# Moving twelve of sixteen modulation weight blocks into the first projections of a GLA and forgetting-attention step

## The reference

```python
def ada_params(c, w, b, n):
    mod = jax.nn.silu(c) @ w + b
    return jnp.split(mod[:, None, :], n, axis=-1)
...
shift, scale, gate = ada_params(c, ada_w[layer], ada_b[layer], 3)
h = rms_norm(x) * (1 + scale) + shift
```

## Time and profile before

| | us |
|---|---|
| median of 3 runs | 3111.63 (3107.04 to 3114.2) |
| the profiled execution | 3111.56 |
| its span, first to last instruction | 3110.0 |
| TensorE busy | 2840.9 (91%) |
| DVE, ACT, POOL busy | 1485.1, 965.3, 790.9 |
| mean granted TensorE clock | 0.95 of full |

### The profile page before, as it was taken

The page is one execution under the profiler, slowest core; times in us unless marked ns, Lnnn a source line. Parts: engine busy times, 40 slices in busy tenths (PEclk is TensorE's granted clock), DMA queues, the critical chain, the costliest instruction groups (busy, mean ns, idle before and its releaser), DMA issues. The chain is left out here.

```text
span 3110.0 us, 41239 instructions
## 1 busy us (share of the span) xinstructions
PE 2840.9 (91%) x15730; PEld 2026.1 (65%) x15730; DVE 1485.1 (48%) x3498; ACT 965.3 (31%) x1579; POOL 790.9 (25%) x460
## 2 busy tenths in 40 slices
PE   4699999997999986999969999699999999994998
PEld 2377777775777865778857877455555555552667
DVE  2462332112877637541166105566666666653343
ACT  2321332211655544210043112134444434442000
POOL 1020000000000003000020000278887888785000
PEclk8799999998999998999989999699999999996999
DMA  8712222113566524221142231334314332314764
GB/s 302 272 68 72 81 65 85 72 45 130 171 218 196 163 93 182 82 75 49 48 174 82 49 72 52 94 110 117 92 37 110 113 96 59 91 32 158 223 214 125
DMA packets 281928, 355.22 MB, mean 114 GB/s; under 512 B 40044, under 2 KB 172460, under 8 KB 281681
## 3 DMA queue, kind: packets, MB, share of 16 engines
q1 hardware_dynamic: 279436, 344.30, 35.2%
q0 software_dynamic: 2304, 8.39, 0.8%
HBM read 250.28 MB, written 102.10 MB: 113 GB/s over the span
## 5 line engine op out<-in xcount | busy, mean ns | idle before, releaser
L2339 POOL TENSOR_TENSOR at_p_sum<-at_p_sum,at_p 128x1024 f32<-128x1024 f32 (+3 forms) x264 | 522.2, 1978 | 84.4 <-ACT at_p L2185 61.4
L2185 ACT ACTIVATE at_p<-psum 128x1024 f32<-128x1024 f32 (+1 forms) x320 | 270.2, 895 | 384.0 <-PE psum L2012 380.0
L2236 DVE CUSTOM_DVE_ANT_0 psum<-psum,at_f_wide 128x512 f32<-128x512 f32 (+3 forms) x640 | 376.9, 631 | 0.0
L717 POOL TENSOR_TENSOR kv_h_lo<-kv_aux,kv_h_hi 128x512 fp32r<-128x512 f32 x16 | 24.1, 1508 | 1015.6 <-ACT kv_h_hi L693 984.7
L2092 PE MATMUL psum<-at_p,at_v 128*64 128x512 f32 (+3 forms) x1280 | 270.5, 544 | 0.7 <-ACT at_p L2185 0.7
L806 PE MATMUL psum<-kv_w_hi,kv_h_hi 128*128 128x512 f32 x512 | 201.2, 393 | 13.1 <-DVE kv_w_lo L961 13.1
L806 PE MATMUL psum<-gla_w_hi,gla_h_hi 128*128 128x512 f32 x512 | 201.3, 393 | 10.7 <-DVE gla_w_lo L961 10.7
L808 PE MATMUL psum<-gla_w_hi,gla_h_lo 128*128 128x512 f32 x512 | 203.0, 397 | 0.0
L807 PE MATMUL psum<-gla_w_lo,gla_h_hi 128*128 128x512 f32 x512 | 202.2, 395 | 0.0
L807 PE MATMUL psum<-kv_w_lo,kv_h_hi 128*128 128x512 f32 x512 | 200.3, 391 | 0.0
L808 PE MATMUL psum<-kv_w_hi,kv_h_lo 128*128 128x512 f32 x512 | 200.0, 391 | 0.0
(11 more groups left out here) (431 smaller groups left out, 6111.1 us busy)
## 6 DMA issues: line engine op xcount, KB each, us to landing
mod_w<-in_ada_w SPq DMA_DIRECT2D x12, 2048.0 KB, 15.5
at_f_wide<-F SPq DMA_DIRECT2D x32, 512.0 KB, 5.4
at_page<-in_cache_k SPq DMA_DIRECT2D x32, 512.0 KB, 3.6
gla_w_raw<-in_gla_w_in SPq DMA_DIRECT2D x6, 2048.0 KB, 7.7
mod_x<-in_x_prompt SPq DMA_DIRECT2D x16, 512.0 KB, 15.9
mod_w<-in_kv_ada_w SPq DMA_DIRECT2D x4, 2048.0 KB, 12.3
v_gla<-gla_stage SPq DMA_DIRECT2D x32, 256.0 KB, 2.0
sg_gla<-gla_stage SPq DMA_DIRECT2D x32, 256.0 KB, 2.0
```

Source lines behind the costliest of these rows:

```text
L717: pool.tensor_tensor(part(h_lo, k, G), h_tmp[0], part(h_hi, k, G).bitcast(F32), ALU.subtract)\
L2185: act.activation(p_tile[e % PT][:, :, skip:NB], pair_of(bank_st[e % 2])[:, :, skip:NB], ACT.Exp)\
L2236: op = dve.tensor_tensor_reduce(pair_of(at(n))[:, a, 0:w], pair_of(at(n))[:, a, 0:w], f_wide[:, a, c * NB:c * NB + w], 1.0, -3.0e38, ALU.s ...
L2339: pool.tensor_tensor(p_sum[s][:, :, skip:NB], p_sum[s][:, :, skip:NB], p_tile[e % PT][:, :, skip:NB], ALU.add).then_inc(p_added, 1)
```

## The change

The modulation phase keeps blocks 0 to 3, the GLA layer's shift and scale. The other twelve are loaded and projected within blocks 1 to 4 of the GLA projections, three in each, through `w_raw`, with TensorE products after units 2, 6 and 10 and folds after units 3, 7 and 11, in PSUM bank 7. ACT copies the strips over part of `w_raw`; DVE adds the bias and writes `modT` or gate rows. The biases of the eight turned blocks come by eight loads into a tile `biasT`; gate biases come by a load each. The next projection's weights are loaded after unit 11 of a block rather than after unit 0 (for blocks 2 to 5). In the modulation phase the order of x changes: four tiles, then the next projection and the fold, with no look-ahead from one group of four to the next.

```diff
@@ modulation_phase
+    blocks = g.mod_blocks[0:g.MOD_FIRST]
@@ SP
-                for n in range(DEEP):
-                    load(n)
+                load(0)
+                sp.wait_ge(cleared, 1)
+                sp.dma_start(bias[0:NC, :], g.i.ada_b[0:1, 0:N * NB].broadcast_to([NC, N * NB])).then_inc(bias_loaded, 16)
+                for n in range(N):
                     load_x(n)
...
+                    if n + 1 < N:
+                        load(n + 1)
@@ PE
                 for n in range(N):
+                    for t in range(PER * n, PER * n + PER):
+                        turn_x(t)
                     if n + 1 < N:
                         project(n + 1)
-                    for t in range(PER * n, PER * n + PER):
-                        turn_x(t)
                     turn(n)
@@ DVE
                 for n in range(N):
-                    if n + 1 < N:
-                        gather(n + 1)
                     for t in range(PER * n, PER * n + PER):
-                        if t + 1 < g.NT:
+                        if (t + 1) % PER:
                             scale_x(t + 1)
                         dve.wait_ge(x_turned, 2 * t + 2)
                         dve.tensor_copy(g.xT[:, 4:8, t * P:(t + 1) * P], ps_x[1]).then_inc(x_kept[1], 1)
+                    if n + 1 < N:
+                        gather(n + 1)
                     keep(n)
+                    if n + 1 < N:
+                        scale_x(PER * n + PER)
...
+PROJECT_AT, FOLD_AT = (2, 6, 10), (3, 7, 11)
@@ projection_phase
+            mod_parts, gate_rows, gate_bias = w_raw[:, 0, :], w_raw[0:NC, 1, :], w_raw[0:NC, 2, :]
...
+        def mod_at(n, t, times):
+
+            return 3 * (n - 1) + times.index(t) if gate and 1 <= n <= 4 and t in times else None
+
+        def mod_load(sp, n, m):
+
+            if m % 3 == 0:
+                sp.wait_ge(w_ready, K * (n + 1) + K)
+                sp.wait_ge(s_made, n + 1)
+            w, j = g.mod_blocks[later[m]]
+            sp.dma_start(w_raw[:, :, :], col_blocks(w, j)).then_inc(mod_loaded, 16)
+
+        def mod_rest(sp, m):
+
+            b = later[m]
+            if b in g.mod_gates:
+                sp.wait_ge(mod_projected, m + 1)
+                sp.dma_start(gate_bias, g.mod_bias[b].broadcast_to([NC, NB])).then_inc(gate_bias_loaded, 16)
+            sp.wait_ge(mod_kept, m + 1)
+            if b in g.mod_gates:
+                sp.dma_start(g.mods[:, b * NB:(b + 1) * NB], gate_rows).then_inc(gate_rows_stored, 16)
+                sp.wait_ge(gate_rows_stored, 16 * gates_to(m))
+
+        def mod_project(pe, m):
+
+            pe.wait_ge(mod_loaded, 16 * m + 16)
+            if m:
+                pe.wait_ge(mod_kept, m)
+            in_strips(pe, g.bank[7], lambda k: g.cT[:, k, :], lambda k: w_raw[:, k, :]).then_inc(mod_projected, 1)
+
+        def mod_part(act, m):
+
+            act.wait_ge(mod_projected, m + 1)
+            act.activation(mod_parts, g.bank[7][:, :], ACT.Copy).then_inc(mod_parted, 1)
+
+        def mod_fold(pe, m):
+
+            pe.wait_ge(mod_parted, m + 1)
+            if later[m] in g.mod_gates:
+                mm = pe.matmul(g.bank[7][0:STRIP, :], g.fold[:, :], mod_parts, start=True, stop=True)
+            else:
+                for q in range(R):
+                    mm = pe.matmul(g.bank[7][:, q * NC:(q + 1) * NC], mod_parts[:, q * P:(q + 1) * P], g.fold[:, 0:NC],
+                                   start=True, stop=True)
+            mm.then_inc(mod_folded, 1)
+
+        def mod_keep(dve, m):
+
+            b = later[m]
+            dve.wait_ge(mod_folded, m + 1)
+            if b in g.mod_gates:
+                dve.wait_ge(gate_bias_loaded, 16 * gates_to(m))
+                dve.tensor_tensor(gate_rows, g.bank[7][0:NC, :], gate_bias, ALU.add).then_inc(mod_kept, 1)
+            else:
+                at = turned_blocks.index(b) * R
+                dve.wait_ge(mod_bias_fixed, 2)
+                dve.tensor_tensor(modT[:, b * R:(b + 1) * R, :], g.bank[7][:, 0:R * NC].rearrange("p (q c) -> p q c", c=NC),
+                                  biasT[:, at:at + R].unsqueeze(2).broadcast_to([P, R, NC]), ALU.add).then_inc(mod_kept, 1)
@@ SP, store_units
+                        if mod_at(p.base + j, t, FOLD_AT) is not None:
+                            m = mod_at(p.base + j, t, FOLD_AT)
+                            mod_rest(sp, m)
+                            if m % 3 < 2:
+                                mod_load(sp, p.base + j, m + 1)
+                            elif p.base + j + 1 < n_blocks:
+                                load_w(*all_blocks[p.base + j + 1])
@@ SP, prologue
                 if gate:
                     z_load(sp)
+                    for n, b in enumerate(turned_blocks):
+                        sp.dma_start(biasT[:, n * R:(n + 1) * R].rearrange("p (o q) -> p o q", o=1),
+                                     g.mod_bias[b].rearrange("a (q p) -> p a q", p=P),
+                                     allow_slow_non_contiguous=True).then_inc(mod_bias_loaded, 16)
                 sp.dma_start(x_in[0][0:NS, :], x_sample).then_inc(x_loaded[0], 16)
@@ PE, block_units
+                        if mod_at(n, t, FOLD_AT) is not None:
+                            mod_fold(pe, mod_at(n, t, FOLD_AT))
+                        if mod_at(n, t, PROJECT_AT) is not None:
+                            mod_project(pe, mod_at(n, t, PROJECT_AT))
```

More of the change, by code:

```diff
@@ L89, in modulation_phase @@
         c_silu = sb("c_silu", [NC, D])
[L90 removed]
+        cT, fold = g.cT, g.fold
         bias = sb("bias_rows", [P, N * NB])
[L92 removed]
         w_in = [sb(f"mod_w{u}", [P, K, NB]) for u in range(DEEP)]
         parts = [sb(f"mod_parts{u}", [P, NB]) for u in range(2)]
[L95 removed]
         c_loaded, bias_loaded, cleared = g.sem("c_loaded"), g.sem("bias_loaded"), g.sem("mod_cleared")
@@ L128, in _ @@
                 sp.dma_start(c_rows[1:NC, :], g.i.c_sample).then_inc(c_loaded, 16)
-                for n in range(DEEP):
-                    load(n)
+                load(0)
+                sp.wait_ge(cleared, 1)
+                sp.dma_start(bias[0:NC, :], g.i.ada_b[0:1, 0:N * NB].broadcast_to([NC, N * NB])).then_inc(bias_loaded, 16)
+                for n in range(N):
                     load_x(n)
[L132 to L144, removed]
-                for u in range(2):
-                    sp.wait_ge(rows_stored[u], 16 * len(gate_blocks) // 2)
+                    if n + 1 < N:
+                        load(n + 1)
             @block.scalar
@@ L212, in turn @@
                                        fold[:, 0:NC], start=True, stop=True)
-                    if n in gate_blocks:
-                        i = gate_blocks.index(n)
-                        if i >= 2:
-                            pe.wait_ge(rows_ready, i - 1)
-                        mm = pe.matmul(ps_gate[i % 2][0:STRIP, :], fold[:, :], parts[n % 2][:, :], start=True, stop=True)
                     mm.then_inc(folded, 1)
@@ L772, in _, with upcoming @@
                             .then_inc(part_loaded[G], 16)
+                all_blocks = [(p, j) for p in plan for j in range(p.blocks)]
+                def upcoming(p, j):
+                    n = p.base + j - 1
+                    if gate and 1 <= n <= 4:
+                        mod_load(sp, n, 3 * (n - 1))
+                    else:
+                        load_w(p, j)
                 def stores(p, j):
@@ L2761, in build @@
             g.logf_all = until_attention("logf_all", [P, g.NT * g.HB])
-            with ExitStack() as kept:
-                g.xT = kept.enter_context(nc.sbuf_tensor("x_turned", [P, K, T], F32))
-                run(modulation_phase)
-            with ExitStack() as kept:
-                g.xT_lo = kept.enter_context(nc.sbuf_tensor("gla_h_lo", [P, K, T], F32R))
-                run(gla_projections)
+            with ExitStack() as both:
+                g.cT = both.enter_context(nc.sbuf_tensor("cT", [P, K, STRIP], F32))
+                g.fold = both.enter_context(nc.sbuf_tensor("fold", [P, STRIP], F32))
+                with ExitStack() as kept:
+                    g.xT = kept.enter_context(nc.sbuf_tensor("x_turned", [P, K, T], F32))
+                    run(modulation_phase)
+                with ExitStack() as kept:
+                    g.xT_lo = kept.enter_context(nc.sbuf_tensor("gla_h_lo", [P, K, T], F32R))
+                    run(gla_projections)
             run(gla_phase)
```

56 lines of the change are left out of this document (31 added, 25 removed).

## The result

The changed kernel takes a median of 3075.97 us (3075.72, 3075.97 and 3078.43; a fourth execution took 3534.93 us at a mean granted clock of 0.766 in place of 0.957 to 0.958 and is left out), beside 3110.55 us before on the same chip: a ratio of 0.9882, 95% interval 0.9866 to 0.9898. In a second session it took 3078.1 us, ratio 0.9896 (0.9874 to 0.9917). The profiled execution took 3075.97 us with a span of 3074.4. The forecast was 3088, 3077 to 3104.

What follows compares the result with a forecast made beforehand. It took the modulation stage as bound by transfers and TensorE as full in blocks 1 to 4. The sum: 3111.6 - 70.2 (stage) + 7 (prologue) + 38.4 (added products) + 1 (waits) = 3088 us, range 3077 to 3104.

Steps and rivals of the forecast that it cites:

- the first stage: Modulation stage: fewer weight loads let the next stage start at 69.1 us, not 139.25; minus 70.2 us (minus 77 to 57).
- the prologue: Start of the first projections: eight bias loads ahead of the sample rows add 7 us (3.7 to 14.7), uncovered.
- I take the middle, 67.6: Modulation stage: its end put midway between 61.4 us and 74.3 with the low clock level throughout.
- I take 7, by the row with the nearest size and count: Projections' prologue: 4,096 bias elements priced at the sample stores' 1.8 ns each, 7.5 us, taken as 7.
- eight take 3.7: Projections' prologue, low end: issue on SP alone, from four loads of 128 elements in 1.84 us; 3.7 us for eight.
- The blocks: Projection blocks 1 to 4: twelve added projections and folds on a full TensorE, plus 38.4 us, and plus 1 for waits.
- the tight place in block 1: Block 1: the gate's bias load follows 4-byte sample-row stores, putting the second weight load at the edge; 1 us (0 to 5).
- shifted by about 23 us and nothing else: Expected sign: everything from the stage after the projections on moves by about 23 us, otherwise unchanged.
- (a): Modulation stage stays at the low clock level, ending at 74.3 us: 3094, or 3100; chance 0.21 shared with the weight-load rival.
- (b): Blocks 1 to 4: TensorE waits for weight loads, gate chains 3 to 4 us late: 3098; chance 0.21 shared with low-clock rival.
- (c): Projections' prologue: bias loads go one column at a time, 67 us, giving 3148; decides from 31 us; chance 0.08.
- (d): Modulation stage keeps its length because the chain of x already set it; the added 46 us stay: 3158; chance 0.03.

Runs made afterwards that it cites:

- the second pair of profiles: The unchanged-before kernel and the changed kernel, each profiled once more without edits; the span fell by 33.1 us from one to the other.
- one_weight_load: Changed kernel with only block 0's weights loaded in the modulation stage and used for all four projections (wrong results); 3077.53 us.
- bias_behind: Changed kernel with the eight bias loads issued behind the sample rows and the first projection weights; median 3073.22 us, ratio 0.9867.
- bias_twice: Changed kernel with the eight bias loads issued a second time, into a second tile, ahead of the sample rows; 3086.92 us.
- closer: Changed kernel with added projections after units 2, 5 and 8 and folds after 3, 6 and 9, three units apart; 3098.38 us.

## Why the prediction was too high, and what of it held

The mechanism held: a stage bound by transfers became one bound by the chain of x, and twelve products and folds of known price joined a full TensorE. Two terms of the sum were mis-sized, on the same side: the first stage, -77.0 us and not -70.2, and the prologue, +4.4 and not +7.

**The first stage: the step "I take the middle, 67.6" failed.** (The middle of 61.4 and 74.3 is 67.85; that slip is 0.3 us.) The chain itself came out as added up for 2.4 GHz: first transposes at 19.1 (18.1 forecast), groups of 10.8 to 11.6 us (11.5), the last work on DVE over at 61.2 (61.4), and 1.1 us to the first transfer (1.5). The -77 named as a bound is what was measured, 6.8 us more than the -70.2 taken; in the second pair of profiles it is -74.5, 4.2 us more. So 2.6 of the 6.8 us differ between two pairs of executions, and the rest is the step: none of the eleven stages in the table ends near the 69.1 taken, the latest at 66.66.

The middle was chosen because TensorE's clock before showed both levels. After shows both as well: the granted clock from 19 to 41 us was 0.84 and 0.69. But the low level fell mostly on transposes of tiles that TensorE has to await from ACT and DVE anyway, and hardly on projections and folds, where nothing else runs. At 0.84 the group took 10.79 us, no more than one at 1.00 without waits for loads (one_weight_load). At 0.69 it took 11.6: 0.8 us more, nearly all from the third tile's transposes to the projection, 3.80 us in place of 3.04, since the projection follows the last tile's transposes at once. The sum had put every instruction of TensorE at the low level into the chain, 15.1 us for a group. An average clock doesn't price a stage; what matters is on which instructions the low level falls.

**The prologue: the term of 7 us measured 4.4.** The step "I take 7, by the row with the nearest size and count" failed: it priced the loads by the number, at the 1.8 ns of the 4-byte stores. Issue on SP is the price (bias_behind takes all but 0.3 us of it away, bias_twice pays it again), and it goes by the load, hardly by the number: 0.55 us for a load of 512 numbers, where the four loads of 128 ahead of them took 1.87 us, 0.47 each. Of the three rows that the prediction weighed, the issue row, "eight take 3.7", was nearest. The Trainium skill, "DMA: Bandwidth & Descriptors", section "Bandwidth", gives about 10.5 ns per packet, measured on transfers issued from GpSimd. An estimate from that figure, 86 us for the 8,192 numbers of bias_twice, doesn't hold for these loads, which SP issues: the trace has 8.7. The loads land 2.2 to 2.6 us after issue.

**The blocks: 39.4 forecast, 38.6 measured.** The prices carried over from the sample product and fold to 0.02 us, and the tight place in block 1, priced at 1 us (0 to 5), is one wait of 1.4 for the reason given. TensorE idle before an added projection was named as a sign that the forecast is wrong; this wait is one, and the sum had a price for it.

**The later phases: "shifted by about 23 us and nothing else".** They are shifted by 34 us, and attention differed by 3.1 in the pair compared, within what it differs between executions of kernels that share its code; no step of the prediction stands behind that part. The range's low end stacked full clock, cheap bias loads and cheap folds, 11 us below the forecast; the time fell 12 us below it, and 13 by the ratio, for the range had no room for such a spread beside them.

**The rivals.** (a) The low level throughout: not in any of the eleven executions. (b) Waits for weights: 1.4 us; closer shows the rival real at one unit less, 14.1 us. (c) Slow bias loads: 4.4 us, and not the 31 from which it would decide. (d) A stage that isn't shortened: it is 77 us shorter, and one_weight_load shows that transfers no longer set its length.

The terms that failed add up: 6.8 (stage) + 2.6 (prologue) + 0.8 (blocks) + 1.6 (later phases) = 11.8 of the 12.0 us between the forecast and the profiled execution; the rest is the rounding of 3087.8 to 3088. In the second pair they are 4.2, 2.6, 0.8 and 1.7.

## What to carry to other kernels

Weight blocks that a full TensorE needs later are loaded for nothing beside its work, if the distance between their products holds the whole round of result, store and load; measure that distance, since one unit less cost 14 us of waits here, and some 5 us more at the lower clock level right behind them. When a stage shows both clock levels, price it twice and look for the instructions that the chain waits for, such as the border projections and the transposes just ahead of them here: there the lower level costs time, and the mean clock of the stage doesn't tell. Small loads ahead of the first one that the next phase waits for cost their issue time on the queue in full, so put the awaited load first; count the loads, not their numbers.

## What the runs showed of the hardware

Loads of 512 single 4-byte numbers cost 0.55 us each to issue, sixteen in a row as well as eight, and loads of 128 cost 0.47. Four stores of 1,024 such numbers took 6.37 us in the kernel before: 0.30 us for the first, up to 2.54 for a later one. Behind the 2 MB weight load the same bias loads were slower to issue: in bias_behind four took 5.13 us and the fifth 2.04, in place of 0.55 each, with nobody waiting. After waits of 8.3 and 4.4 us in a full stream (closer), TensorE's next product ran at the lower level, 3.64 us; after one of 1.4 it took 1.92. Phases that no edit touches differ between the thirteen profiles by 3 us (attention, 866.2 to 869.3) and by 7.6 (output, 263.3 to 270.9). The two shortest output phases, 263.3 and 264.7, are those of the two kernels with extra transposes some 2.7 ms earlier; what links them, if anything does, stays open. A gain of a few microseconds can't be read from one such phase of one profile.
